# Hybrid decoder block on eight cores: norm factor in PSUM, later modulation sums, second token tile loaded and scaled ahead of w_ada

## What is computed

```python
mod = (silu(c) @ w_ada + b_ada)[:, None, :]
sh1, sc1, ga1, sh2, sc2, ga2 = split(mod, 6)
h = rms_norm(x, g_mix) * (1 + sc1) + sh1
z = h @ w_in + b_in                       # q, k, v, conv_b, conv_c, conv_x, gate_a, gate_c
attn = sliding_window_sink_attention(q, k, v, sinks)      # 16 query heads, 2 kv heads, window 128
conv = conv_b * causal_depthwise_conv(conv_c * conv_x, conv_w)   # 3 taps
merged = sigmoid(gate_a) * attn + sigmoid(gate_c) * conv
x = x + ga1 * (merged @ w_out)
h = rms_norm(x, g_ffn) * (1 + sc2) + sh2
g, u = split(h @ w_ffn_in, 2)
x = x + ga2 * ((silu(g) * u) @ w_ffn_out)
out = rms_norm(x, g_final)
```

## Time and profile before

| | us |
|---|---|
| median of three runs | 1089.92 |
| lowest and highest run | 1057.12, 1121.12 |
| profiled execution, its own time | 1056.61 |
| its span, slowest core (core 0) | 1054.5 |
| span of the fastest core (core 3) | 1040.8 |

### The profile page before, as it was taken

One profiled execution on the slowest core, in us unless ns is written; L12 is line 12 of the kernel. 1 busy time (PEld: TensorE's weight loads), 2 busy tenths in 40 slices (PEclk: granted clock), 3 DMA queues, 4 the chain that ended last, 5 costly groups with the idle time before them and its releaser, 6 DMA issues.

```text
span 1054.5 us, 15358 instructions; the slowest of 8 cores (1040.8 to 1054.5 us)
## 1 busy us (share of the span) xinstructions
PE 961.6 (91%) x5474; PEld 452.4 (43%) x5571; DVE 585.1 (55%) x829; ACT 385.6 (37%) x592; POOL 209.1 (20%) x282
## 2 busy tenths in 40 slices
PE   0469999999979999999998999999999999999993
PEld 0335444444434444444443444444444444444443
DVE  1247858586857877878868531234212244253656
ACT  4166545454535454545266531100111100233233
POOL 2100222222211212121563410000100001023213
PEclk9989999999989999999998999999999999999997
DMA  9970462855244434032800432210522202110222
GB/s 191 226 175 1 60 111 29 125 96 81 48 53 128 91 130 91 11 56 36 136 16 11 71 57 44 40 21 1 91 40 40 40 1 47 23 66 15 80 80 81
DMA packets 44651, 72.26 MB, mean 69 GB/s; under 512 B 19600, under 2 KB 21904, under 8 KB 42528
## 3 DMA queue, kind: packets, MB, share of 16 engines
q0 software_dynamic: 21600, 45.36, 27.1%
q1 hardware_dynamic: 22976, 25.91, 8.1%
HBM read 108.15 MB, written 8.45 MB: 111 GB/s over the span
## 4 chain that ended last, share of the span: by engine, by line
PE 78%; DVE 8%; DMA 6%; issue 4%; ACT 2%; POOL 1%; DVEq 0%; ACTq 0%; POOLq 0%; SPq 0%
PE psum L968 28%; PE psum L593 27%; PE psum L981 14%; DMA wadaB<-w_ada_l 5%; PE psum L911 3%; PE psum L745 3%; DVE rden L770 2%; PE psum L721 2%; DMA mc<-mscr 1%; DVE h L928 1%; DVE h L543 1%; DVE cv L668 1%; DVE nrm L771 1%; DVE pT L733 1%; PE psum L531 0%
## 5 line engine op out<-in xcount | busy, mean ns | idle before, releaser
L593 PE MATMUL psum<-h,ws 128*128 128x512 bf16 (+1 forms) x1694 | 366.0, 366 | 15.7 <-issue 5.7
L968 PE MATMUL psum<-h,fws 128*128 128x512 bf16 x1380 | 306.1, 380 | 6.0 <-ACT rs L473 4.5
L593 PEld LDWEIGHTS psum<-h,ws 128*128 128x128 bf16 x1744 | 161.4, 99 | 188.6 <-issue 38.6
L968 PEld LDWEIGHTS psum<-h,fws 128*128 128x128 bf16 x1408 | 138.0, 98 | 173.3 <-issue 9.4
L976 DVE TENSOR_TENSOR mg<-psum,sg 128x512 bf16<-128x512 f32 x88 | 60.4, 688 | 196.5 <-PE psum L968 189.6
L973 ACT ACTIVATE sg<-psum 128x512 bf16<-128x512 f32 x88 | 52.1, 596 | 307.6 <-PE psum L968 297.6
L981 PE MATMUL psum<-mg,fwo 128*128 128x512 bf16 (+1 forms) x747 | 152.4, 363 | 1.7 <-DVE mg L976 1.0
L770 DVE RECIPROCAL rden<-rden 128x256 f32<-128x256 f32 x64 | 111.9, 1749 | 12.6 <-ACT rden L768 11.6
L988 DVE SCALAR_TENSOR_TENSOR xres<-psum,modc,xres 128x512 f32<-128x512 f32 (+1 forms) x104 | 73.7, 709 | 78.3 <-PE psum L981 77.5
L981 PEld LDWEIGHTS psum<-mg,fwo 128*128 128x128 bf16 x760 | 74.3, 98 | 79.2 <-issue 1.5
L784 POOL TENSOR_TENSOR mg<-nrm,cv 128x256 bf16<-128x256 f32 x64 | 53.8, 840 | 273.8 <-DVE cv L690 141.4
(11 more groups left out here) (89 smaller groups left out, 679.1 us busy)
## 6 DMA issues: line engine op xcount, KB each, us to landing
ws<-w_in_l POOLq DMA_DIRECT2D x50, 256.0 KB, 5.7
fws<-w_fi_l POOLq DMA_DIRECT2D x44, 256.0 KB, 4.7
wadaB<-w_ada_l POOLq DMA_DIRECT2D x20, 512.0 KB, 6.8
xres<-xtok SPq DMA_DIRECT2D x8, 1024.0 KB, 11.8
xres<-xt SPq DMA_DIRECT2D x8, 1024.0 KB, 6.0
out<-xres SPq DMA_DIRECT2D x12, 512.0 KB, 2.6
fwo<-w_fo_l POOLq DMA_DIRECT2D x22, 256.0 KB, 5.0
wadaA<-w_ada_l POOLq DMA_DIRECT2D x4, 512.0 KB, 19.2
```

What stands on the lines that cost most here:

```text
L593: P.op("pe", [lambda e, k=k: e.matmul(bank(b)[:, 0:n], lhsT=WS[s * 1024 + k * 128, s * 1024 + (k + 1) * 128], rhs=hk(k, col, n), start=(k ...
L968: P.op("pe", [lambda e, k=k, w=w, wo=wo, b=b: e.matmul(bank(b), lhsT=w[wo + k * 128, wo + (k + 1) * 128], rhs=hk(k, 128 + tt * 512, 512), ...
```

## The change

- `mods_rows`: the matmuls are planned 5 us, the sum behind the read-back 25 us after they could first run, and their planned cost is 1.05 instead of 0.8.
- `rstd_of` is given a bank, 6 or 7 in turn by tile. Those two leave the rotation of the output projection and the FFN, which is now banks 0 to 5. Where a whole tile, or the last half tile, is normed, the reciprocal is written back into that bank and the products read it there. The products of the second norm of tiles 1 and 2 have a priority of 16 instead of 9 steps behind.
- Tile 1 of x is issued on SP right behind the halo, ahead of everything of w_ada in time. A second buffer `xn1` (over the bytes of the conv buffers `cx` and `tg` and the start of `rden`) takes tiles 1 and 3. Tile 1 is squared, scaled and transposed ahead of the modulation; its first two transposed pieces lie in banks 0 and 1, the others take banks 2 and 3 from the rotation, and all are emptied right behind tile 0's and the halo's.
- The first eight weight slots and the mask are issued without a wait for tile 1. Tile 2 waits for the fifth weight slot, tile 3 for tile 2.
- In the first channel group `prep(2)` follows tile 0's groups, and `prep(3)` the conv groups of tile 1. `turned(2)` lies between those, `turned(3)` in front of the conv groups of tile 2.
- Both modulation vectors of the start use bank 2. Two helpers that nothing calls are gone.

The diff, cut to its core (... marks what is left out):

```diff
...
+    XN1 = buf("xn1", A_AT + 28704, 4096, BF16)
...
+        load_x(1, xtok_d)
         def load_wada(v, st, parts=4, after=(), only=None):
...
-        for zi in range(4):
+        for zi in range(8):
-        x1 = load_x(1, xtok_d, after=(wa_parts[1],))
-        for zi in range(4, 8):
-            load_z(zi, after=(x1,))
-        P.op("pool", lambda e: e.dma_start(out=MASK.t[:], in_=msk_d[:, 0:896]), writes=[MASK.iv()], dma="d_msk", cost=0.6, nbytes=458752,
-             after=(x1,))
-        x2 = load_x(2, xtok_d, after=(x1,))
+        P.op("pool", lambda e: e.dma_start(out=MASK.t[:], in_=msk_d[:, 0:896]), writes=[MASK.iv()], dma="d_msk", cost=0.6, nbytes=458752)
+        x2 = load_x(2, xtok_d, after=(P.sem_prev["d_ws4"],))
...
-        def rstd_of(total, n, sd, slack=1.5):
-            b = nb()
+        def rstd_of(total, n, sd, slack, b, in_psum):
             P.op("pe", [lambda e: e.matmul(bank(b)[:, 0:n], lhsT=ONESF.t[:], rhs=total[0][total[1], total[1] + n], start=True, stop=True)],
-            P.op("dve", lambda e: e.reciprocal(out=d[o + n, o + 2 * n], in_=d[o, o + n]),
-                 reads=[d.iv(o, o + n)], writes=[d.iv(o + n, o + 2 * n)], cost=0.1 + n * 0.0066)
+            P.op("dve", lambda e: e.reciprocal(out=bank(b)[:, 0:n] if in_psum else d[o + n, o + 2 * n], in_=d[o, o + n]),
+                 reads=[d.iv(o, o + n)], writes=[pv_(b)] if in_psum else [d.iv(o + n, o + 2 * n)], cost=0.1 + n * 0.0066)
...
         def stats(src, a, nblk, s0, out, engs=("act",)):
...
-        def turn(xn, nblk, hcol, bks, engs):
+        def turn(xn, nblk, hcol, bks, engs, only=None):
-            for g in range(8 // per):
+            for g in range(8 // per) if only is None else only:
                 P.op("pe", [lambda e, j=j, i=i, g=g, tp=tp: e.transpose(tp[:, j * n + i * 128:j * n + (i + 1) * 128],
...
         def prep(tt):
-            stats(X, tt * 4096, 4, 1 + 4 * tt, XN, ("act", "dve") if tt == 1 else ("act", "act", "act", "dve"))
+            xn = XN if tt == 2 else XN1
+            stats(X, tt * 4096, 4, 1 + 4 * tt, xn, ("act", "act", "act", "dve"))
-            scale(X, tt * 4096, 4, 1 + 4 * tt, XN, ("dve",) * 4 if tt == 1 else ("dve", "act", "dve", "dve"))
+            scale(X, tt * 4096, 4, 1 + 4 * tt, xn, ("dve", "act", "dve", "dve"))
         def turned(tt):
-            turn(XN, 4, 128 + 512 * tt, None, ("dve",))
+            turn(XN if tt == 2 else XN1, 4, 128 + 512 * tt, None, ("dve", "act") if tt == 2 else ("dve",))
+        stats(X, 4096, 4, 5, XN1, ("act", "dve"))
+        roots(5, 4)
+        scale(X, 4096, 4, 5, XN1, ("dve", "act", "dve", "act"))
         def mods_cols(v, st, half):
-            b = nb()
+            b = 2
             for k in range(8):
                 P.op("pe", [lambda e, k=k, j=j: e.matmul(bank(b)[:, j:j + 1], lhsT=st[k * 1024 + j * 128, k * 1024 + (j + 1) * 128],
...
-        turn(XNH, 1, 0, None, ("dve",))
+        turn(XNH, 1, 0, (3,), ("dve",))
+        turn(XN1, 4, 640, (0, 1), ("act", "dve"), (0, 1))
+        rot[0] = 1
+        turn(XN1, 4, 640, None, ("dve", "act"), (2, 3))
         uses = {zi: 4 for zi in range(NZ + 8)}
...
-                     reads=[WA[1].iv(), SCREP.iv()], writes=[pv_(b)], cost=0.8)
+                     reads=[WA[1].iv(), SCREP.iv()], writes=[pv_(b)], cost=1.05, lat=5.0)
...
-                 reads=[MC4.iv(mo, mo + 32)], writes=[MODC.iv(v * 8, v * 8 + 8)], cost=0.2)
+                 reads=[MC4.iv(mo, mo + 32)], writes=[MODC.iv(v * 8, v * 8 + 8)], cost=0.2, lat=25.0)
...
-                    if t < 3:
-                        seq.append(lambda t=t: prep(t + 1))
-                    if t < 3:
-                        seq.append(lambda t=t: turned(t + 1))
-                    if t > 0:
-                        seq += conv[max(2, cut[t - 1]):cut[t]]
+                        seq.append(lambda: prep(2))
+                    elif t == 1:
+                        seq += conv[2:4]
+                        seq.append(lambda: turned(2))
+                        seq += conv[4:6]
+                        seq.append(lambda: prep(3))
+                    else:
+                        if t == 2:
+                            seq.append(lambda: turned(3))
+                        seq += conv[cut[t - 1]:cut[t]]
...
         def second_norm(tt):
-            rstd_of((ACC, (tt % 2) * 512), 512, (RS, ro))
-            P.prio = pos[0] + 9
+            sb = 6 + tt % 2
+            rstd_of((ACC, (tt % 2) * 512), 512, (RS, ro), 1.5, sb, True)
+            P.prio = pos[0] + (16 if tt in (1, 2) else 9)
             for k in range(8):
-                P.op("dve", lambda e, a=a, k=k: e.tensor_tensor(out=hk(k, 128 + 512 * tt, 512), in0=X[a, a + 512], in1=RS[ro + 512, ro + 1024], op=ALU.mult),
-                     reads=[X.iv(a, a + 512), RS.iv(ro + 512, ro + 1024)], writes=[H.iv(k * NTH + 128 + 512 * tt, k * NTH + 640 + 512 * tt)],
-                     cost=dve_us(512))
+                P.op("dve", lambda e, a=a, k=k: e.tensor_tensor(out=hk(k, 128 + 512 * tt, 512), in0=X[a, a + 512], in1=bank(sb), op=ALU.mult),
+                     reads=[X.iv(a, a + 512), pv_(sb)], writes=[H.iv(k * NTH + 128 + 512 * tt, k * NTH + 640 + 512 * tt)],
+                     cost=dve_us(512, 1, True))
             for k in range(8):
...
         def finish_tile(tt, lo, n, i, on_dve=()):
-            rstd_of((ACC, (i % 2) * 512), n, (RS, ro), 1.5 if n == 512 else 0.0)
+            sb = 6 + i % 2
+            on_bank = len(on_dve) == 8 or n == 512
+            rstd_of((ACC, (i % 2) * 512), n, (RS, ro), 1.5 if n == 512 else 0.0, sb, on_bank)
-                rs = RS[ro + n, ro + 2 * n]
-                io = dict(reads=[X.iv(a0, a1), RS.iv(ro + n, ro + 2 * n), cst_iv], writes=[X.iv(a0, a1)])
+                rs = bank(sb)[:, 0:n] if on_bank else RS[ro + n, ro + 2 * n]
+                io = dict(reads=[X.iv(a0, a1), pv_(sb) if on_bank else RS.iv(ro + n, ro + 2 * n), cst_iv], writes=[X.iv(a0, a1)])
...
-        banks[:] = [4, 5, 6, 7, 0, 1, 2, 3]
+        banks[:] = [0, 1, 2, 3, 4, 5]
```

More of the change, by code:

```diff
@@ L474, in rstd_of @@
                  reads=[pv_(b), EPSC.iv()], writes=[d.iv(o, o + n)], cost=act_us(n))
-            P.op("dve", lambda e: e.reciprocal(out=d[o + n, o + 2 * n], in_=d[o, o + n]),
-                 reads=[d.iv(o, o + n)], writes=[d.iv(o + n, o + 2 * n)], cost=0.1 + n * 0.0066)
-        def scaled(src, a, n, rs, hcol, eng):
-            d, o = rs
-            P.op(eng, lambda e: e.tensor_tensor(out=h3[:, :, hcol:hcol + n], in0=src[a, a + 8 * n].rearrange("p (k t) -> p k t", k=8),
-                                                in1=d[o, o + n].rearrange("p (o t) -> p o t", o=1).to_broadcast([128, 8, n]), op=ALU.mult),
-                 reads=[src.iv(a, a + 8 * n), d.iv(o, o + n)], writes=h_iv(hcol, n),
-                 cost=dve_us(8 * n) if eng == "dve" else pool_us(8 * n))
-        def affine(hcol, n, acol, shcol, ivs):
-            for k in range(8):
-                P.op("dve", lambda e, k=k: e.tensor_scalar(out=hk(k, hcol, n), in0=hk(k, hcol, n), scalar1=acol[:, k:k + 1],
-                                                           scalar2=shcol[:, k:k + 1], op0=ALU.mult, op1=ALU.add),
-                     reads=ivs + [H.iv(k * NTH + hcol, k * NTH + hcol + n)], writes=[H.iv(k * NTH + hcol, k * NTH + hcol + n)],
-                     cost=dve_us(n, 4))
+            P.op("dve", lambda e: e.reciprocal(out=bank(b)[:, 0:n] if in_psum else d[o + n, o + 2 * n], in_=d[o, o + n]),
+                 reads=[d.iv(o, o + n)], writes=[pv_(b)] if in_psum else [d.iv(o + n, o + 2 * n)], cost=0.1 + n * 0.0066)
         def stats(src, a, nblk, s0, out, engs=("act",)):
```

## The result

The changed kernel takes 1040.9 us, median of four runs (1040.1 to 1113.4), the kernel before 1073.5, median of four (1057.0 to 1121.1). Some executions of either kernel are several per cent longer, on cores of one die with a lower granted clock; without them the ratio is 0.9845 (95% interval 0.9821 to 0.9868). That is 1.55% faster: clear of the spread of the runs, and under the 2% at which the prediction drew its line between faster and the same. The profiled execution took 1040.1 us, against 1056.6 before.

The account below looks back on a forecast made before the run. TensorE is full from 577 to 1023 us, so only its earlier idle or low-clock holes can pay. Core 2 ends slowest: 1048.9 - 3.9 - 2.8 - 6.1 = 1036.1, with 2.1 around it 1038 us; range 1028 to 1053.

Parts of the forecast that it names:

- part 2: Later modulation sums: waits for read-back and w_ada go, 9.5 us on core 0, 2.8 on core 2, nothing on core 3.
- part 1: Start, tile 1 ahead of w_ada: later first projection, fuller 58 to 74.5 us; gains 5.6 us on core 0, 3.9 on 2 and 3.
- part 3: Norm factor in its own banks: wait for the Sqrt and slow matmuls go, 7.1 us less 1 charged, gain 6.1.
- halo's V chain: Start: table loads and two ScalarE evictions still behind tile 0's groups; 2 us charged, of 0 to 5.
- The hole at tile 2: TensorE near 78 us: tile 2's h is ready with a margin of 2 us; 1 us charged, of 0 to 5.
- tile 2 is late: Rival: tile 2 lands 5 us behind 67.8, costing 5 us and about 2 at the lower clock: 1045; chance 0.18.
- an idle of over 1 us away from 78: Sign: from the first projection to 100 us TensorE has no idle of over 1 us, except near 78.
- the edits left over: Tile 2's transposes on two engines, squaring engines, removed helpers: work moves between engines idle 30% or more, at no cost.
- the sums' waits stay: Rival: w_ada's landing varies by more than 5 us, so modulation waits remain: 1040 to 1045; chance 0.10.
- the charge for the new queue: Second-norm products queued later on VectorE with a six-bank rotation: 5.9 us for eight, below 8.6; 1 us charged.
- New waits of projections for an eviction near 540 to 600 would show the banks at fault: Sign for the rival that six banks are too few: 1045 to 1050 if only norm stretches suffer; chance 0.10.
- All holes close: Rival: all holes go, also the V chain, and the cores meet at core 3's: 1028 to 1033; chance 0.14.

Follow-up runs that it names:

- experiment 4: Changed kernel with the modulation matmuls planned as before (cost 0.8, no 5 us), the sum still 25 us behind its read-back: 1039.8 us, 0.9826.
- the last kernel: Changed kernel with the whole reciprocal queued 8 steps later, the modulation matmuls' old plan, and the sum planned for 12 us instead of 25: 1035.4 us, 0.9791.
- experiment 1: Kernel before with one part of the change at a time: part 2 1054.9 us, part 3 1055.1, part 1 1053.2.
- part 2 alone: Kernel before with only the later modulation sums (matmuls cost 1.05 and 5 us, sum 25 us): 1054.9 us, 0.9968.
- experiment 3: Changed kernel with the last two transposed pieces of tile 1 behind tile 0's projections: 1041.7 us, 0.9853.
- experiment 5: Changed kernel with the norm factor kept in SBUF, sums still in banks 6 and 7, rotation still six banks: 1040.8 us, 0.984.
- the first kernel of experiment 8: Changed kernel with the second norm's reciprocal in halves, 8 steps later, and the modulation matmuls planned as before: 1035.8 us, 0.979.

## Why the prediction was right and wrong

The forecast of 1038 us lies 2.9 under the measured median and 2.1 under the profiled execution (1040.1). Its change of -1.8% was made against the profiled 1056.6; measured are -1.55%. The median of 1090 us shown before was no base for the change, as the text said. The sum for core 2 came out nearly right and those for the others did not, and its terms show that this was luck: errors cancelled (part 2 below).

| term, gain in us | forecast core 0 / 2 / 3 | measured core 0 / 2 / 3 |
|---|---|---|
| part 1 (start to group 1) | 5.6 / 3.9 / 3.9 | 4.5 / 4.2 / 1.2 |
| part 2 (group 1 to output projection) | 9.5 / 2.8 / 0 | 6.9 / 3.9 / -1.7 |
| part 3 (output projection to end) | 6.1 / 6.1 / 6.1 | 5.0 / 5.4 / 3.7 |
| end of the core's span, us | 1033.3 / 1036.1 / 1030.8 | 1038.2 / 1035.5 / 1037.6 |

**Part 1: right, in its steps.** The last w_ada part moved from 41.1 to 45.9 us on the mean of the cores, by 4.8 for 4.6. The first projection moved by 5.2, 6.0 and 7.8 us on cores 0, 2 and 3 (forecast 4.3, 6.0, 6.0). Behind it core 0 regained 9.7 us for 9.9. For the halo's V chain 2 were charged, and what is left there is a wait of 1.4 us for ScalarE's eviction of K. The hole at tile 2 (0.6 us) was charged 1. The rival "tile 2 is late" fell. One sign failed: the 1.4 us at 64 are an idle of over 1 us away from 78. And the edits left over were said to load only engines "idle 30% or more", but ScalarE is busy 19.95 of 25.5 us from 74.5 to 100 in the earlier trace rows, idle 22%. Core 3 alone is off: its sum, at 40.3 us before, is at 46.8 now, 6.5 later where the mean over the cores is 4.8.

**Part 2: the first step that failed.** "With 25 us planned for the read-back and 5 for the sums, all of it goes: 9.5 us on core 0, 2.8 on core 2, nothing on core 3" took the waits away and charged nothing for the new places. Measured are 6.9, 3.9 and a loss of 1.7. Three things were mis-sized. First, the 5 us planned in front of the modulation row and the 25 in front of the sum cost each quiet core 2.6 us from group 1 to 5: 1.6 to 1.8 from the matmuls' plan (experiment 4), about 0.5 from the sum's (the last kernel), and 0.3 left. 0.9 comes back behind group 5. I had written that only the next w_ada part waits later. Second, the losses themselves. Against a quiet core (208.3 us) core 0 lost 8.5 us in this stretch and not 9.5, and core 2 lost 5.6 and not 2.8. On core 2, then, too small a loss and no charge offset each other, and core 2 was to set the time. Third, the loss of a core was read from one execution as if it belonged to the core. It moves, as the repeats in experiment 1 show. The mechanism was right: the waits went, the sums did it (part 2 alone makes all eight cores equal), and "the sums' waits stay" fell.

**Part 3: the second step that failed, the charge for the new queue.** The 4.00 us wait for the root and its slow matmuls went. The products came down to 680 ns, none over 687 on any core (forecast: below 760). But two terms were mis-sized. The holes were worth more than 7.1: with the reciprocal out of the way the median core gains 8.7 (535.9 to 527.2). And the new wait took 4.0 of it, not 1, at another instruction than the one I charged. The step that failed is the sentence that twice or half the reciprocal's time "would lie on a VectorE that is busy 166.8 of 446 us". Its time was as before, 3.36 us. It was its place, in front of six evictions, that stopped TensorE for 3.0 us and left eight matmuls slow. The share quoted was also that of another stage, the FFN from 577 us on; from 530 to 550 VectorE is busy 17.0 of 20 us in the changed kernel. And a mean idle share says nothing about one queue in order. "New waits of projections for an eviction near 540 to 600 would show the banks at fault" named the sign rightly and the cause wrongly: five banks cost nothing, and moving the reciprocal gave 4.0 us (531.2 to 527.2) with six. Whether eight banks would have hidden the reciprocal in that place was not tried.

**All holes close** (1028 to 1033) was not reached by any kernel here. The best are four that can't be told apart, at 1035.4 to 1036.0 us. The simplest is the change with the whole reciprocal queued 8 steps later, 1035.6 us: 2.1% under the kernel before, and 5 us under the changed one.

**Left open.** Why the landing of w_ada's parts differs by some 2 us from core to core, and whether the 3.0 us at the start (the last piece of tile 1 waits for a bank that VectorE empties) can be had: experiment 3 moved that piece and won nothing. The 4.5 to 4.7 us that TensorE waits for the last norm's sum at the end are in all kernels, and nothing was tried against them.

## What to carry to other kernels

When an edit takes a wait away, look at what the instruction is queued ahead of in its new place; price it by the queue at that moment, not by the engine's idle share over the stage. When several cores run the same program and the slowest sets the time, read a wait that only some cores show as a chance that each core has, and value an edit on the quiet cores as well, where it can only cost. A planned latency is an insurance: a plan of 12 us left room for every read-back seen, and 25 cost the quiet cores half a microsecond more.

## What the hardware showed that I had not expected

- The collision of a two-SBUF-input VectorE product with GpSimd slows both (experiment 5): from 686 up to 1756 ns on VectorE, from 1274 up to 2447 ns on GpSimd. I had reckoned with the VectorE side only.
- A reciprocal of 128x512 f32 takes 3.36 us into PSUM and 3.35 into SBUF. The output's place has no price here.
- The small read-back of the sums took 4.1 to 8.4 us on core 0 of the changed kernel and up to 11.6 on its core 7, up to 11.0 in the last kernel, 12.03 on core 0 and 13.3 on core 7 before, and 14.9 once in the first kernel of experiment 8, for the same bytes. The median of a core was 4.2 to 7.2.
